# Bidirectional gated delta scan: products of a tile made once for both directions in two of six chunks

## The reference, cut to what matters

```python
decay = jnp.exp(jnp.where(incl, gc[..., :, None] - gc[..., None, :], -jnp.inf))
a_low = jnp.where(strict, jnp.einsum('nbhcd,nbhsd->nbhcs', kb, kc) * decay, 0.0)
tmat = a_low + jnp.eye(C, dtype=f32)
...
qk = jnp.einsum('nbhcd,nbhsd->nbhcs', qc, kc) * decay
kd = kc * jnp.exp(g_last[..., None] - gc)[..., None]
def step(s, inp):
    w_i, u_i, qk_i, qg_i, kd_i, gl_i = inp
    v_new = u_i - jnp.einsum('bhcd,bhde->bhce', w_i, s)
    o = jnp.einsum('bhcd,bhde->bhce', qg_i, s) + jnp.einsum('bhcs,bhse->bhce', qk_i, v_new)
    s = s * jnp.exp(gl_i)[..., None, None] + jnp.einsum('bhcd,bhce->bhde', kd_i, v_new)
```

## Time and profile before

| | |
|---|---|
| median of 3 runs | 1705.09 us |
| profiled execution | 1704.45 us, its span 1702.3 us |
| mean granted TensorE clock | 0.983 |
| PE busy | 1618.2 us, 95% of the span |
| DVE busy | 734.4 us, 43% |
| ACT busy | 466.6 us, 27% |
| POOL busy | 569.8 us, 33% |

### The profile page before, as it was taken

One profiled execution on the slowest core, in us unless ns is written; L12 is line 12 of the kernel. 1 busy time (PEld: TensorE's weight loads), 2 busy tenths in 40 slices (PEclk: granted clock), 3 DMA queues, 4 the chain that ended last, 5 costly groups with the idle time before them and its releaser, 6 DMA issues. The chain is left out here.

```text
span 1702.3 us, 36038 instructions
## 1 busy us (share of the span) xinstructions
PE 1618.2 (95%) x14725; PEld 1108.7 (65%) x14725; DVE 734.4 (43%) x1515; ACT 466.6 (27%) x1042; POOL 569.8 (33%) x698
## 2 busy tenths in 40 slices
PE   6999999889999999999999999999979999999998
PEld 4577875557887865555556447786668986555544
DVE  4257543345545451121111546744456675224233
ACT  4212433253333131111111231253353322111111
POOL 2656304226566213111110155611538881000000
PEclk9999999999999989999999999999989999999999
DMA  9330100069884249999999302010220035899995
GB/s 337 91 115 26 50 15 28 13 191 289 253 269 176 75 176 338 372 359 360 357 342 344 110 25 75 25 50 17 63 85 24 15 124 209 336 413 407 411 413 227
DMA packets 160358, 323.73 MB, mean 190 GB/s; under 512 B 30153, under 2 KB 118127, under 8 KB 144879
## 3 DMA queue, kind: packets, MB, share of 16 engines
q1 hardware_dynamic: 127584, 287.20, 45.8%
q0 software_dynamic: 7008, 21.74, 4.6%
q10 hardware_dynamic: 25646, 13.12, 2.8%
HBM read 307.31 MB, written 14.71 MB: 189 GB/s over the span
## 5 line engine op out<-in xcount | busy, mean ns | idle before, releaser
L1531 PE MATMUL psum<-ring,arena 128*64 128x256 f32 x1536 | 172.8, 381 | 6.8 <-DVE arena L3131 3.4
L1531 PEld LDWEIGHTS psum<-ring,arena 128*64 128x64 f32 x1536 | 108.6, 137 | 68.3 <-issue 13.4
L3642 POOL DMA_INDIRECT big<-h_rows_lat,idx x16 | 15.7, 981 | 346.1 <-PE psum L1664 174.0
L802 PE MATMUL psum<-hT,ring 128*128 128x256 f32 (+2 forms) x496 | 130.2, 421 | 0.0
L3152 DVE TENSOR_TENSOR arena<-arena,psum 128x384 f32<-128x384 f32 (+1 forms) x32 | 15.6, 487 | 257.6 <-PE psum L1540 158.5
L802 PEld LDWEIGHTS psum<-hT,ring 128*128 128x128 f32 (+1 forms) x496 | 92.7, 188 | 36.9 <-issue 26.6
L3190 DVE SCALAR_TENSOR_TENSOR xT<-psum,modraw,xT 128x512 f32<-128x512 f32 (+1 forms) x136 | 79.7, 621 | 48.6 <-PE psum L1618 33.8
L975 PE MATMUL psum<-hT,ring 128*128 128x256 f32 (+1 forms) x192 | 80.0, 525 | 0.0
L2444 ACT COPY arena<-psum 128x512 f32<-128x512 f32 (+2 forms) x49 | 23.7, 483 | 202.5 <-PE psum L1553 143.4
L1614 PE MATMUL psum<-arena 128*128 128x512 f32 x144 | 65.8, 602 | 4.4 <-DVE arena L3177 2.7
L2754 DVE TENSOR_REDUCE small<-psum 128x1 f32<-128x768 f32 (+1 forms) x40 | 33.9, 849 | 82.3 <-PE psum L996 82.2
(11 more groups left out here) (476 smaller groups left out, 3771.7 us busy)
## 6 DMA issues: line engine op xcount, KB each, us to landing
ring<-in_moe_w_gate SPq DMA_DIRECT2D x64, 1024.0 KB, 9.6
ring<-in_ada_w SPq DMA_DIRECT2D x48, 1024.0 KB, 7.1
ring<-in_moe_w_up SPq DMA_DIRECT2D x32, 1024.0 KB, 10.3
hT<-in_moe_w_down SPq DMA_DIRECT2D x24, 1024.0 KB, 12.7
ring<-in_w_in SPq DMA_DIRECT2D x20, 1024.0 KB, 5.5
big<-in_moe_w_up SPq DMA_DIRECT2D x16, 1024.0 KB, 10.9
sz<-in_moe_w_down SPq DMA_DIRECT2D x16, 1024.0 KB, 12.5
big<-in_moe_w_down SPq DMA_DIRECT2D x16, 1024.0 KB
```

The source lines that it names most:

```text
L802: m = pe.matmul(b[0:c1 - c0, 0:n], lhsT=w[:, k, c0:c1], rhs=hT[:, k, t0:t0 + n], start=k == 0, stop=k == KD - 1)
L1531: m = pe.matmul(b[e * CAP_L:(e + 1) * CAP_L, 0:2 * P], lhsT=xs[:, k, e, 0:CAP_L], rhs=w[e][:, 2 * (k - ks[0]) + q, :], start=k == 0, stop= ...
```

## The change

`SHARED` names, for each layer, the products that are kept from the fourth chunk for the fifth: "kk" in the first layer; "kk", "kr" and "qk" in the second. For chunk 3 (the fourth) PE makes them as before, ACT copies each from PSUM into a part of `mixT` that nothing else uses at the time, and DVE reads the copy. For chunk 4 (the fifth) PE makes nothing, and DVE reads the other direction's copy. PSUM's bank is freed by ACT's copy, and what waited for DVE's reading of the bank now waits for a count on the semaphore "comb".

```diff
--- before.py
+++ after.py
@@ -95,6 +95,7 @@
     (("kr", 0), ("kr", 1), ("kk", 0)), (("ks", 0), ("ks", 1)), (("kk", 1), ("t0", 0), ("qk", 0), ("qk", 1)))
 G_SLOTS = (3, 5)
 GATES, SUMS, ROWS, LANES_EXP = (2, 1), (6, 3), (8, 4), (11, 7)
+SHARED = ((("kk", 3),), (("kk", 3), ("kr", 3), ("qk", 3)))
 ADA_SLOTS = ((0, 1, 0, 1, 1, 1, 2), (1, 1, 1, 1, 1, 1, 0))
 
 
@@ -310,11 +311,11 @@
 
         def tokens_made(eng, l):
 
-            eng.wait_ge(sems[l]["comb"], l * (1 + IN_PAIRS) + 1)
+            eng.wait_ge(sems[l]["comb"], sum(1 + IN_PAIRS + len(shared_steps(x)) for x in range(l)) + 1)
 
         def taps_added(eng, l, q):
 
-            eng.wait_ge(sems[l]["comb"], l * (1 + IN_PAIRS) + 2 + q)
+            eng.wait_ge(sems[l]["comb"], sum(1 + IN_PAIRS + len(shared_steps(x)) for x in range(l)) + 2 + q)
 
         def middle_taps(l):
 
@@ -540,6 +541,35 @@
                     out.append((what, i, d))
             return out
 
+        def shared_steps(l):
+
+            order = [x for j in range(NT) for slot in range(len(BETWEEN)) for x in between(j, slot)]
+            return [(what, i, d) for what, i, d in order for w, j in SHARED[l] if what == w and i in (j, j + 1)]
+
+        def kept(l, what, j, d):
+
+            i = tile_of(d, j)
+            row, col = 2, {"kr": (2, 5), "qk": (3, 4)}.get(what, (0, 1))[i] if i < CT else i
+            if i >= CT and what != "kk":
+                row, col = GH * (what == "qk"), i - CT - 1
+            return mixT[:, row:row + GH, col * P:(col + 1) * P]
+
+        def product_kept(l, what, j):
+
+            return (what, j) in SHARED[l]
+
+        def product_shared(l, what, j):
+
+            return (what, j - 1) in SHARED[l]
+
+        def factor_made(eng, l, what, j, d):
+
+            if product_kept(l, what, j) or product_shared(l, what, j):
+                base = sum(1 + IN_PAIRS + len(shared_steps(x)) for x in range(l)) + 1 + IN_PAIRS
+                eng.wait_ge(sems[l]["comb"], base + shared_steps(l).index((what, j, d)) + 1)
+            else:
+                evacuated(eng, (what, l, j, d))
+
         def ada_at(j, slot):
 
             counts = ADA_SLOTS[min(j, 1)]
@@ -1044,6 +1074,8 @@
                     i = tile_of(d, j)
                     t = slice(i * P, (i + 1) * P)
                     use_o = need_ctx or i >= CT
+                    if product_shared(l, what, j):
+                        return
                     if what == "g" and j == 0:
                         heads(("g", l, j, d), lambda o, h: pe.matmul(
                             o, lhsT=gb[:, 0, i, d * GH + h:d * GH + h + 1].to_broadcast([P, P]), rhs=tri[:, d, :],
@@ -1082,7 +1114,7 @@
                         if j:
                             pe.wait_ge(s["qg"], row_products(l, j) + 2 + d + 1)
                         evacuated(pe, ("v", l, j, d))
-                        evacuated(pe, ("qk", l, j, d))
+                        factor_made(pe, l, "qk", j, d)
                         for h in range(GH):
                             o = b[:, h * P:(h + 1) * P]
                             if j:
@@ -1091,7 +1123,7 @@
                         done(m, ("go", l, j, d))
                     elif what == "st" and j < NT - 1:
                         evacuated(pe, ("v", l, j, d))
-                        evacuated(pe, ("kr", l, j, d))
+                        factor_made(pe, l, "kr", j, d)
                         heads(("st", l, j, d), lambda o, h: pe.matmul(
                             o, lhsT=gKD[d][:, h, :], rhs=gV[d][:, h, :], start=True, stop=True))
 
@@ -2204,7 +2236,7 @@
                     act.wait_ge(s["gr%d" % d], 16 * j)
                     if j >= 2:
                         act.wait_ge(s["eb"], 2 * (j - 2) + d + 1)
-                        evacuated(act, ("kr", l, j - 2, d))
+                        factor_made(act, l, "kr", j - 2, d)
                     if j >= 3:
                         act.wait_ge(s["sdec"], 2 * (j - 3) + d + 1)
                     e, q = gE[j % 2][d], gQG[j % 2][d]
@@ -2240,6 +2272,10 @@
 
                 def gdn_between(j, slot):
 
+                    for what, i, d in between(j, slot):
+                        if product_kept(l, what, i):
+                            b = product_ready(act, (what, l, i, d)).rearrange("p (h c) -> p h c", h=GH)
+                            read_out(act.copy(kept(l, what, i, d), b), (what, l, i, d))
                     if slot in (1, 2) and 1 <= j < NT - 1:
                         decay_rows(j + 1, slot - 1)
                     if slot in G_SLOTS and 1 <= j < NT - 1:
@@ -2773,6 +2809,23 @@
                 dve.wait_ge(s_sum, 16)
                 gX, gXC, gAO = lent_views(l)
 
+                def heads_product(what, j, d):
+
+                    if product_shared(l, what, j):
+                        return kept(l, what, j, d)
+                    if product_kept(l, what, j):
+                        evacuated(dve, (what, l, j, d))
+                        return kept(l, what, j, d)
+                    return product_ready(dve, (what, l, j, d)).rearrange("p (h c) -> p h c", h=GH)
+
+                def factor_done(ins, key):
+
+                    what, _, j, d = key
+                    if product_shared(l, what, j) or product_kept(l, what, j):
+                        ins.then_inc(s["comb"], 1)
+                    else:
+                        read_out(ins, key)
+
                 def gdn_piece(what, j, d):
 
                     i = tile_of(d, j)
@@ -2785,7 +2838,7 @@
                         read_out(dve.tensor_tensor(gE0[l][d], b, g1.unsqueeze(2).to_broadcast([P, GH, P]),
                                                    ALU.subtract), key)
                     elif what == "kk":
-                        b = product_ready(dve, key).rearrange("p (h c) -> p h c", h=GH)
+                        b = heads_product(what, j, d)
                         dve.wait_ge(s["eb"], 2 * j + d + 1)
                         if j:
                             dve.wait_ge(s["ml"], 2 * j)
@@ -2796,17 +2849,17 @@
                             dve.tensor_tensor(a[rows_of[1 - r], d, GH:2 * GH, :], b[c, :, c], decay[c, :, c], ALU.mult)
                         c, r = rows_of[d], rows_of[1 - d]
                         dve.tensor_tensor(gAO[j % 2][c, 0:2, :], b[r, 0:2, c], decay[r, 0:2, c], ALU.mult)
-                        read_out(dve.tensor_tensor(gAO[j % 2][r, 2:4, :], b[r, 2:4, c], decay[r, 2:4, c], ALU.mult), key)
+                        factor_done(dve.tensor_tensor(gAO[j % 2][r, 2:4, :], b[r, 2:4, c], decay[r, 2:4, c], ALU.mult), key)
                     elif what == "qk" and use_o:
-                        b = product_ready(dve, key)
+                        b = heads_product(what, j, d)
                         dve.wait_ge(s["dm"], 2 * (j - j_out) + d + 1)
-                        x = gE[j % 2][d].rearrange("p h c -> p (h c)")
-                        read_out(dve.scalar_tensor_tensor(out=x, in0=b, scalar=-1.0, in1=x, op0=ALU.mult, op1=ALU.mult),
-                                 key)
+                        x = gE[j % 2][d]
+                        factor_done(dve.scalar_tensor_tensor(out=x, in0=b, scalar=-1.0, in1=x, op0=ALU.mult, op1=ALU.mult),
+                                    key)
                     elif what == "kr":
-                        b = product_ready(dve, key).rearrange("p (h c) -> p h c", h=GH)
+                        b = heads_product(what, j, d)
                         dve.wait_ge(s["dex"], 2 * j + d + 1)
-                        read_out(dve.scalar_tensor_tensor(
+                        factor_done(dve.scalar_tensor_tensor(
                             out=gKD[d], in0=b, scalar=-1.0,
                             in1=gt4[:, j % 2, d, 0, :].unsqueeze(2).to_broadcast([P, GH, P]), op0=ALU.mult,
                             op1=ALU.mult), key)
@@ -2820,6 +2873,12 @@
                     elif what == "go" and use_o:
                         b = product_ready(dve, key).rearrange("p (h c) -> p h c", h=GH)
                         o = mixT[:, 2:2 + GH, i * P:(i + 1) * P]
+                        if j == 2:
+                            for e in range(2):
+                                factor_made(dve, l, "kr", 1, e)
+                        if j == 3:
+                            for e in range(2):
+                                factor_made(dve, l, "kk", 4, e)
                         first = [tile_of(1 - d, x) for x in range(NT)].index(i) > j
                         if first:
                             read_out(dve.tensor_scalar(o, b, -1.0, None, ALU.mult), key)
@@ -3418,7 +3477,7 @@
                     for d in range(2):
                         pool.wait_ge(s["dex"], 2 * j + d + 1)
                         if j:
-                            evacuated(pool, ("kk", l, j - 1, d))
+                            factor_made(pool, l, "kk", j - 1, d)
                         i = tile_of(d, j)
                         pool.tensor_tensor(gEB[d] if j else gEB0[l][d], gE[j % 2][d] if j else gE0[l][d],
```

(2 more changed lines are left out.)

## The result

The changed kernel's median is 1718.24 us (1716.03 to 1719.77, four runs) against 1704.77 us (1704.38 to 1706.93, four runs) of the kernel before beside it: ratio 1.007, 95% interval 1.0057 to 1.0083, +13.5 us by the medians and +11.9 us by the ratio. On another chip the same kernel gave 1.0061 (1.0044 to 1.0079). It is slower, as forecast, but by about twice the 5.8 us forecast. The profiled execution took 1716.03 us, 11.6 us above that of before. Four of all the timed runs, of 1748 to 3768 us, were in a slower state of the chip; no ratio counts them.

What follows compares the result with a forecast made beforehand. The prediction took a DVE and POOL chain of 21.3 us a turn to bound the second layer; meetings of 1.5 + 1.6 + 0.9 + 0.9 + 0.9 = 5.8 us on the median 1705.09 gave 1710.9 us, range 1703.5 to 1714.0.

Steps and rivals of the forecast that it cites:

- PE's removed work: Second layer: up to 4.8 us of products leave PE, counted as no gain because DVE's and POOL's chain covers them.
- DVE and POOL block each other: Second layer's third to fifth chunks: DVE products with both operands in SBUF meet POOL instructions, 5.8 us lost in sum.
- Third turn: Second layer, third chunk: DVE's key products meet POOL's second L3423 and its four copies, 1.5 us lost.
- Fourth turn, transposes, second keys and queries: Second layer, fourth chunk: 1.6 us lost at transposes and the keys behind them, 0.9 us where queries meet the masks.
- Fifth and sixth: Second layer, fifth chunk's terms: transposes meeting two POOL instructions lose 0.9 us, queries meeting the masks another 0.9 us.
- The 2 us that I had worked out from the other page's 58 and 120 cycles: Second layer: cheaper fixed part of DVE's SBUF reads might return about 2 us, making the sum +3.8 us; not adopted.
- So the clock takes nothing from the argument.: Whole kernel: mean granted clock 0.983, both stretches read at 1.00 (2.4 GHz), so no clock term entered the sum.
- becomes idle time ahead of L1147 and L1089: Second layer: work leaving PE turns into PE idle time before levels and outputs, counted as 0 us.
- has no PE work in it: Second layer's scan: the 21.3 us loop of DVE, POOL and hand-overs contains no PE work; PE fills 97% of it.
- The first layer is worth 0: First layer: gain of at most 2.0 us against delays through ACT and POOL; range -2.0 to +1.5 us, taken as 0.
- ACT: Second layer: copies delay ACT's later work by 0.6 to 1.2 us; taken as 0, up to 1 us a turn.
- Rival 3: Second layer: copies make ACT the new wait, 1 us in each of three turns, +8.8 us, 1713.9 us; chance 13%.

Runs made afterwards that it cites:

- quarter_made: Kernel before, PE making only the first of four heads of each shared product in the second layer's fifth chunk: 1707.04 us, 1.001.
- pe_filled: Changed kernel, PE making the fifth chunk's shared products again into a bank nobody reads: 1716.46 us, 1.0054 of the kernel before.
- warm_beside: Changed kernel with PE's long waits in the second layer's scan filled by unread matmuls, repeated beside the unfilled changed kernel: 1713.62 us, 1.0044 of the kernel before.
- after_warm: Changed kernel with unread matmuls ahead of PE's waits for v and the masks in the second layer's scan: 1713.51 us, 1.006 of the kernel before.
- sbuf_read: Kernel before, DVE taking one operand from unfilled SBUF instead of PSUM in the second layer's fourth and fifth chunks: 1716.49 us, 1.0049.
- sbuf_warm: sbuf_read plus three unread 128x512 matmuls ahead of PE's 2.86 us wait in the third turn: 1713.75 us, 1.0048 of the kernel before.
- layer1_alone_c: Changed kernel with only the second layer sharing its products, the first as before: 1717.93 us, 1.0064 of the kernel before.
- sbuf_quarter: Kernel before with the edits of sbuf_read and quarter_made together, without ACT copies: 1716.53 us, 1.0051.
- after: The changed kernel as first measured and profiled, against the kernel before: median 1718.24 us, 1.007.
- keys_by_copy: Changed kernel with the second layer sharing only its key products, so both layers share keys by copy: 1707.25 us, 1.0 of the kernel before.
- sbuf_queries: Kernel before, DVE taking only the query products of the second layer's fourth and fifth chunks from unfilled SBUF: 1709.84 us, 1.0026.

## Why the prediction was right in kind and wrong in size

- **PE's removed work is worth nothing in the second layer.** Right. quarter_made leaves the turns and the clock unchanged, and pe_filled, with the work put back, is not slower than the changed kernel.
- **DVE and POOL block each other, and the sum of it is 5.8 us.** Right, term by term: with the clock held the scan is 5.5 us longer (warm_beside, and after_warm again). Third turn 1.43 us (I had 1.5). Fourth turn, transposes, second keys and queries, 2.29 us (1.6 + 0.9 = 2.5). Fifth and sixth, 1.51 + 0.33 us (0.9 + 0.9). The masks that meet L2857 take up to 1.17 us instead of 0.73, the 0.44 us more that I took from the earlier trace rows. I had read the rule of the Trainium skill ("SBUF — State Buffer", Who interferes with whom), that the loser fully blocks, as a loss of the whole 0.65 us. That was a misreading: POOL's mask at 1323.01 starts when 0.59 us of DVE's product are left (1322.81, 0.79 us long), so a full block costs at most that rest, and 0.44 does not speak against the rule. That POOL and DVE contend with two inputs in SBUF and not with one, as the page says, sbuf_read bears out: one operand moved from PSUM cost some 8 us. The 2 us that I had worked out from the other page's 58 and 120 cycles ("VectorE: DVE Perf Modes", The TRN2 errata) were not seen: the quiet key products take 0.27 to 0.30 us for 64x128 from either memory.
- **"So the clock takes nothing from the argument."** This is the step that failed. I read the clock of the kernel before, 1.00 in both stretches, and took it for a property of the stretch, so the sum has no term for it. The meetings make PE's waits longer, and I priced only the meetings' own length. In these turns the clock fell to 1.2 GHz behind each wait of 2.3 to 2.9 us, and behind some of 1.4 to 2.2 us; v and the outputs take up to twice their time, and POOL's L3533 waits 5.5 us for the outputs. In the scan that is 4.2 us in the first profile (9.76 less 5.55) and some 3 us in the second (10.1 less 5.5, less the 1.5 us of DVE's squares); the medians of the pair differ by 3.9 us. It was not what leaves PE: that this "becomes idle time ahead of L1147 and L1089" at no price was right taken alone (quarter_made, clock 1.00), and the clock falls with all of the work there (sbuf_read, pe_filled). The Trainium skill has the rule ("TensorE: Matmul & The Clock Gate", Part 1: The HAM clock gate): the chip gates PE's clock by how busy PE has lately been. The traces agree, with 1.00 in the filled scan and 0.91 in the unfilled one. It spoke against the longer waits, and I had not weighed it.
- **The chain of DVE and POOL "has no PE work in it".** True at full clock only. L3474 waits for PE's outputs; before, PE was just in time for it (1.4 us of waits for PE over the scan).
- **The first layer is worth 0.** Right: 0.9995.
- **ACT.** I took 0 for its delay. Right for the third and fourth turn, as far as one profile of each kernel shows: DVE's transposes did wait 1.72 us for the copy, but with the clock at 1.00 these turns are as long without copies (sbuf_warm) as with them (warm_beside), within 0.1 us. The 2 us between layer1_alone_c and sbuf_quarter are within their intervals, and 1.5 us between their profiled scans is the dear form of the squares.
- **About 2 us behind the scan.** In the profile of after they come with the clock at 0.66 at the start of the experts, behind waits of 2.15 us (a DMA; 0.62 in the kernel before) and 1.60 us. Seen only; no experiment held the clock there, and I had no term for it.

Rival 3 came nearest in time (1713.9 us) with the wrong mechanism; the true one, a clock that falls behind the longer waits, was no rival of mine. With my 5.8 us and the measured 4 us of clock in the scan it would have stood at 1715 us, still 3 us short of the median.

## What to carry to other kernels

A granted clock of 1.00 in the kernel before is no constant of the kernel after. Where a change makes other engines slower, look at how much longer PE's waits get, and at who waits for PE behind them: here the waits went from 1.5 to 2.5 us and the scan lost 3 to 4 us beyond what it loses with the clock held. Less work on PE alone did nothing of the kind (quarter_made). And before an operand is moved from PSUM to SBUF for DVE, look at what POOL does at that moment: alone the move was free here (1.29 us for two of 128x512 either way), beside POOL the two transposes took 3.13 us. A kernel with 95% of PE busy can still be bound by two other engines; leaving out part of PE's work is a quick test.

## What the runs showed of the hardware beyond that

Over 243 timed runs of all the kernels here, the time goes with the mean granted clock within one and the same kernel: deviations from the kernel's own mean have a correlation of -0.71, and 0.001 less of clock goes with 1.04 us more. The kernel before alone (94 runs) spreads over 0.0016 of clock and 2.3 us, one standard deviation each. So about half of the variance within a kernel goes with the clock (a third in the kernel before alone, correlation -0.60); which of them is the cause the runs don't show. keys_by_copy and after_warm spread most, 15 us between their fastest and slowest run.

A meeting of DVE and POOL has two outcomes. With starts 0.04 us apart (1.64 and 1.68 us behind POOL's first instruction), the changed kernel's squares on DVE took 2.14 us in one profile and 3.63 us in another. The Trainium skill ("SBUF — State Buffer", Who interferes with whom) says that issue order decides who blocks; the traces agree in that each of the two can be the loser (POOL 5.06 instead of 4.13 us, DVE 3.02 instead of some 0.69). They don't agree in the order: in sbuf_queries DVE's instruction starts at 1367.02 and stands behind three of POOL's that start later, at 1367.42, 1368.10 and 1368.78.

Filling one wait of several was not enough here: in sbuf_warm it gave 1.6 us back in its turn, and a fall turned up two turns later. Filling all the long waits (after_warm, warm_beside) left none in the scan.
